# Router logits from the raw residual, with the scaled router weight stationary in four column groups

## The chip, the cores and the metric

The kernel runs on one core of one Trainium2 chip. It is one program that computes the whole two-layer encoder trunk. The metric is the device time of one execution in microseconds (us), as the median of three runs. TensorE is called PE, VectorE DVE, ScalarE ACT, GpSimd POOL and SyncE SP in the profile. PE does matrix products and writes them to PSUM; the other engines read PSUM and work on SBUF; SP and POOL start most transfers.

## The reference

There are 512 tokens of width 1024, and two layers. All is float32. A layer has an attention half and an expert half. What matters here is the end of the first half and the router at the head of the second:

```
x = x + g1 * hybrid_mixer(...)                        # residual after the mixer
h = rms_norm(x, norm2[l]) * (1.0 + sc2) + sh2         # x * rsqrt(mean(x*x) + EPS) * norm2, then scale and shift
scores = sigmoid(h @ w_router)                        # 512 x 16 experts, in 4 groups of 4
biased = scores + router_bias                         # best group by its two best, then the top 2 of it
gw = scores of the two chosen / their sum
each expert: (silu(xb @ w1[e]) * (xb @ w3[e])) @ w2[e]
x = x + g2 * (sum over the two chosen of gw * expert output)
```

`w_router` is 1024 x 16 and the same in both layers. The norm's gain, `sc2` and `sh2` are per channel; the reciprocal root of the mean square is per token. The experts' tokens are gathered by choice and multiplied with three weight tensors of 2 MB each.

## The kernel before, in words

Each engine has its own program, written out by hand, and the programs meet only at semaphores; an engine works its list strictly in order. Tokens are in four blocks (t = 0 to 3) of 128, one token to a partition; the 1024 channels are eight chunks of 128. Matrix products over channels need the tokens with channels on the partitions, so a block is transposed by PE against the identity, eight transposes into two PSUM banks of four, and copied from there to `hT`. The eight chunk transposes of a block are numbered in two counters, `tr_r` (transposed) and `tr_e` (read out of PSUM), which count in order.

*Around the change.* The last part of the attention half is the output product: eight products (k = 0 to 7, that is block t = k // 2, column half n = k % 2), each of eight matmuls of 128x512 (line 1871). Behind each, VectorE multiplies by the gate row and adds to the residual `x` (L1323, L1326), and counts `x1`. When both halves of a block are added:

- ScalarE squares the block and sums (L884; for the last block in two halves, L1031 and L1033), VectorE makes the mean (L1106), ScalarE takes the root (L888), VectorE the reciprocal `rstd` (L1111) and the normed block `xn` (L1113), and counts `xn_s`.
- PE transposes `xn` (L1630, called from L1875 or L1878). ScalarE evacuates it with the channel's scale and shift, one operation a chunk (L896); for the last block VectorE does the second four chunks (L1346).
- PE multiplies for the router: eight matmuls for a block, the block's 128 tokens stationary and the 16 columns of `wr` moving (L1855), into 16 columns of PSUM bank 2. The logits of block t-1 stand in PE's list behind product k = 2t + 1.
- POOL stores each `xn` block to DRAM (L818), waits for all four stores, then for the slot table, and gathers the tokens of the first expert pass (L826).

When all four blocks' logits stand in the bank, `lg_r` is counted. ScalarE takes the sigmoid of all 64 columns in one operation (L1040), VectorE chooses the experts, counts, ranks and makes the table of slots in some sixty small operations (L1359 to L1446), with small PE products in between. Then the gather, transposes and eleven expert passes follow (L1958, L1969). Each pass has 128 rows split into fixed tiles of 32, 64 or 128 rows, given to the experts by the rank of their counts; should an expert have more tokens than its tiles hold, a loop of extra blocks follows the passes.

*SP's queue* loads weights in a fixed order. In this stage: the first expert's weights while the output product runs; then it waits for the expert order (`ord_s`, L618), later for the first gather (L628), for `lg_r` (L634) before the load into `hT`, and for the stores of `xn` (L636) before the load into `reg_a`.

*Before this stage* VectorE's part of the gate loop (lines 1291 to 1317) runs eight rounds with PE and ScalarE. In layer 0 there are also small products for the next layer's modulation in PE's list behind the logits (L1889).

## Time and profile before

| | |
|---|---|
| median of 3 runs | 1590.02 us (1587.45 to 1592.77) |
| span of the profiled execution | 1586.8 us |
| profiled execution's own time | not recorded beyond its span |
| PE busy | 1485.2 us, 94% |
| DVE busy | 572.7 us, 36% |
| ACT busy | 438.6 us, 28% |
| POOL busy | 87.0 us, 5% |
| mean granted PE clock | 0.971 of full speed |
| router products of a block (L1855) | 16 records; 4 blocks, 2 layers |
| moved by DMA | 346.82 MB, mean 219 GB/s |

The profile is of one execution. The span runs from its first to its last instruction. A float32 matmul shows as two records. An engine's busy time says little by itself: what counts is the chain that ended last, followed back from the last instruction to what released it. "Issue" in a row is time in which an engine waited for nothing that the profile shows. The granted clock is the share of the full rate that PE was given in a stretch; 1.00 is 2.4 GHz and 0.50 is 1.2 GHz.

### The profile page before, as it was taken

The page shows a single profiled execution, that of the slowest core. Times are in us where ns is not written, and L with a number is a line of the kernel's source. Part 1 is how long each engine was busy: PE and PEld are TensorE (multiplying, and loading weights), DVE is VectorE, ACT ScalarE, POOL GpSimd, SP SyncE. Part 2 cuts the span into 40 slices and gives each one's busy share as a digit, 9 for nine tenths or more (in the row PEclk, how much of TensorE's full clock was granted, in tenths as well). Part 3 has the DMA queues.
Part 4 walks back from the last instruction along what each step waited for, and adds up shares of the span by engine and source line. Part 5 has one row for each costly group of instructions (what it writes and reads, how often), then busy time and mean ns, then how long its engine had stood idle before and what let it go on. Part 6 is the DMA issues. An engine that isn't in the chain of part 4 may idle for free.

```text
span 1586.8 us, 19587 instructions
## 1 busy us (share of the span) xinstructions
PE 1485.2 (94%) x7552; PEld 813.4 (51%) x7553; DVE 572.7 (36%) x1325; ACT 438.6 (28%) x1020; POOL 87.0 (5%) x96
## 2 busy tenths in 40 slices
PE   5998999999999789999989899999999949999996
PEld 1664555677755433444346555666775533334442
DVE  0056554566642401111154464464332250111115
ACT  2326565300013021211141565541010321121111
POOL 0000002000000001010000000110000000111000
PEclk8999999999999699999999999999999969999998
DMA  9626073225161699999962433401305139999994
GB/s 362 226 82 215 28 245 113 69 67 154 58 252 40 263 419 421 422 422 423 379 240 106 154 117 110 157 1 40 106 0 204 48 116 423 418 420 422 420 410 171
DMA packets 94872, 346.82 MB, mean 219 GB/s; under 512 B 13722, under 2 KB 37882, under 8 KB 80376
## 3 DMA queue, kind: packets, MB, share of 16 engines
q1 hardware_dynamic: 69152, 305.68, 49.2%
q0 software_dynamic: 8976, 31.45, 5.3%
q10 hardware_dynamic: 16648, 8.40, 1.8%
q8 instruction: 62, 1.02, 0.3%
q14 instruction: 34, 0.28, 0.1%
HBM read 331.54 MB, written 21.00 MB: 222 GB/s over the span
## 4 chain that ended last, share of the span: by engine, by line
PE 87%; DMA 5%; DVE 4%; ACT 2%; issue 1%; DVEq 1%; SPq 0%; POOLq 0%; ACTq 0%
PE bank L1958 18%; PE bank L1716 12%; PE bank L1666 10%; PE bank L1969 9%; PE bank L1758 7%; PE bank L1871 7%; PE bank L1773 5%; PE bank L1783 4%; PE bank L1793 4%; DMA ring<-in_w 2%; PE bank L1699 2%; PE bank L1597 2%; PE bank L1630 1%; DMA ring<-in_w_ada 1%; PE bank L1924 1%
## 5 line engine op out<-in xcount | busy, mean ns | idle before, releaser
L1958 PE MATMUL bank<-ring,reg_b 128*32 128x512 f32 (+2 forms) x1376 | 284.1, 607 | 2.9 <-ACT reg_b L1048 2.9
L1958 PEld LDWEIGHTS bank<-ring,reg_b 128*32 128x32 f32 (+2 forms) x1376 | 94.3, 129 | 141.1 <-issue 137.0
L1666 PE MATMUL bank<-ring,hT 128*128 128x512 f32 (+3 forms) x512 | 159.3, 472 | 2.4 <-ACT hT L896 2.4
L1666 PEld LDWEIGHTS bank<-ring,hT 128*128 128x128 f32 x512 | 97.8, 192 | 59.3 <-issue 32.4
L1969 PE MATMUL bank<-ring,reg_b 128*32 128x512 f32 (+2 forms) x576 | 127.3, 594 | 0.0
L1048 ACT ACTIVATE reg_b<-bank,cur 128x128 f32<-128x128 f32 x176 | 64.0, 470 | 180.3 <-PE bank L1924 180.3
L1758 PE MATMUL bank<-reg_a,ring 128*128 128x512 f32 x256 | 112.6, 593 | 0.9 <-issue 0.9
L1871 PE MATMUL bank<-ring,reg_b 128*128 128x512 f32 x256 | 112.2, 593 | 0.0
L975 ACT ACTIVATE reg_f<-bank,nmax 128x512 f32<-128x512 f32 x128 | 87.2, 684 | 61.2 <-DVE nmax L1258 60.1
L1258 DVE TENSOR_REDUCE nmax<-bank 128x1 f32<-128x512 f32 x128 | 83.8, 686 | 50.0 <-PE bank L1773 49.9
L1716 PE MATMUL bank<-hT,ring 128*128 128x256 f32 x384 | 88.1, 379 | 0.0
L1511 DVE TENSOR_TENSOR reg_d<-bank,reg_c 128x512 f32<-128x512 f32 x44 | 30.4, 692 | 145.5 <-PE bank L1969 145.5
L1716 PEld LDWEIGHTS bank<-hT,ring 128*128 128x128 f32 x384 | 72.8, 190 | 15.8 <-issue 6.7
L1501 DVE TENSOR_TENSOR reg_b<-bank,reg_b 128x512 f32<-128x512 f32 x22 | 15.2, 692 | 178.4 <-ACT reg_b L1055 178.4
L1793 PE MATMUL bank<-cst,reg_f 128*128 128x128 f32 x512 | 71.2, 281 | 6.7 <-DVE reg_f L1252 4.1
L1758 PEld LDWEIGHTS bank<-reg_a,ring 128*128 128x128 f32 x256 | 48.5, 190 | 55.6 <-issue 54.9
L1871 PEld LDWEIGHTS bank<-ring,reg_b 128*128 128x128 f32 x256 | 47.9, 190 | 56.4 <-issue 56.4
L1969 PEld LDWEIGHTS bank<-ring,reg_b 128*32 128x32 f32 (+2 forms) x576 | 41.4, 129 | 55.6 <-issue 54.9
L1252 DVE TENSOR_SCALAR reg_f<-reg_f,linv 128x512 f32<-128x512 f32 x128 | 66.2, 517 | 9.9
L1793 PEld LDWEIGHTS bank<-cst,reg_f 128*128 128x128 f32 x512 | 55.3, 141 | 26.3 <-DVE reg_f L1252 16.5
L896 ACT ACTIVATE hT<-bank,cur 128x128 f32<-128x128 f32 x120 | 43.7, 468 | 66.7 <-PE bank L1630 53.3
L1773 PE MATMUL bank<-reg_b 96*128 96x512 f32 x128 | 60.8, 603 | 0.0
(276 smaller groups left out, 1812.8 us busy)
## 6 DMA issues: line engine op xcount, KB each, us to landing
ring<-in_w SPq DMA_DIRECT2D x76, 2048.0 KB, 22.9
ring<-in_w_ada SPq DMA_DIRECT2D x19, 2048.0 KB, 8.0
ring<-in_w_in SPq DMA_DIRECT2D x10, 2048.0 KB, 19.3
hT<-in_w SPq DMA_DIRECT2D x10, 2048.0 KB
reg_a<-in_w SPq DMA_DIRECT2D x10, 2048.0 KB, 22.2
vb<-in_w_ada ACTq DMA_DIRECT2D x16, 512.0 KB, 4.0
ring<-in_w_o SPq DMA_DIRECT2D x4, 2048.0 KB, 8.7
ring<-in_w_proj_a SPq DMA_DIRECT2D x8, 512.0 KB, 10.8
```

The source lines that it names most:

```text
L975: A(prob[:, u % 2, h, :], bank[4 + at][:, :], ACT.Exp, bias=nmax[:, at:at + 1], accum_out=lsum[:, at:at + 1]).then_inc(ex_s, 1)
L1048: ins = A(xsT[:, b, cc, :], bank[(p0 + k) % 2][:, c * P:(c + 1) * P], ACT.Identity, scale=scale2(cc), bias=shift2(cc))
L1252: TS(prob[:, u % 2, h, :], prob[:, u % 2, h, :], linv[:, at:at + 1], None, ALU.mult).then_inc(pn_s, 1)
L1258: v.tensor_reduce(nmax[:, at:at + 1], bank[4 + at][:, :], X, ALU.max, negate=True).then_inc(mx_s, 1)
L1666: ins = pe.matmul(bank[z_bank(k)][:, 0:n], hT[:, c, t * P:(t + 1) * P], w[:, c, :], start=c == 0, stop=c == NC - 1)
L1716: ins = pe.matmul(bank[bk][:, half * 256:(half + 1) * 256], w[:, c, :], tokens[:, c, :], start=c == 0, stop=c == 3)
L1758: ins = pe.matmul(branch_bank(j, q)[:, :], w[:, c, (j % 4) * P:(j % 4 + 1) * P], oT[:, c + 4 * q, :], start=c == 0, stop=c == 3)
L1773: pe.matmul(bank[4 + 2 * (u % 2) + h][:, :], q_of(k, h), k_of(k, h), start=True, stop=True).then_inc(s_r, 1)
L1793: ins = pe.transpose(bank[2 + h][:, kc * P:(kc + 1) * P], prob[:, u % 2, h, kc * P:(kc + 1) * P], ident)
L1871: ins = pe.matmul(wo_bank(k)[:, :], mT[:, c, t * P:(t + 1) * P], w[:, c, :], start=c == 0, stop=c == NC - 1)
L1958: ins = pe.matmul(bank[bk][at:at + n, :], xsT[:, p % 2, c, at:at + n], slot(MOE_SLOT[j, m], NC, F)[:, c, :], start=c == 0, stop=c == NC - 1)
L1969: ins = pe.matmul(bank[6 + h][at:at + n, :], uT[:, c, at:at + n], slot(MOE_SLOT[j, 2], 4, D)[:, c, h * 512:(h + 1) * 512], start=c == 0, s ...
```

## The change

The logits are computed from the residual before its norm. With r the reciprocal root of a token, s and b the channel's scale and shift (s holds the norm's gain), the logits are r * (x @ (s * W)) + b @ W.

- VectorE makes `wr_g`, the router weight times the scale, 16 columns and 16 zero columns for each of the eight chunks, ahead of the gate loop, and the row sums of shift times weight, `wr_sum`, behind it. PE multiplies those by a matrix of ones after the first output product, which gives b @ W on every partition; VectorE copies it to `wr_c`.
- PE transposes `x` itself as soon as a block's residual is added. The copies to `hT` are now plain, of four chunks in one operation: ScalarE for all but the first half of the last block, which is VectorE's.
- The router product has the weight stationary, 32 columns wide, and the tokens moving, 128 columns. Chunk c goes to column group c % 4, so that a bank holds four partial sums on partitions 0, 32, 64 and 96. VectorE copies the 128x128 partials to SBUF. A second product with the partials stationary and a selection matrix of 16 columns (`sum_groups`, new constants) moving adds the four up and turns tokens back to partitions. VectorE then multiplies by r and adds `wr_c`. These steps are spread over the following products for blocks 0 to 2.
- The normed block is still made, for the gather. For blocks 0 to 2 VectorE does it as before; for the last block ScalarE does it, after the sigmoid. ScalarE's wait for `cur2_s` moves behind that.

```diff
+C_SEL = 812
-C_N = 812
+C_N = 828
...
+    for g in range(4):
+        c[32 * g:32 * g + E, C_SEL:C_SEL + E] = np.eye(E, dtype=np.float32)
...
+        logit_p = reg_d[:, 2048:2304].rearrange("p (b n) -> p b n", b=2)
+        logit = reg_d[:, 2304:2304 + NT * E].rearrange("p (t e) -> p t e", t=NT)
+        wr_g = reg_b[:, 4096:4352].rearrange("p (c n) -> p c n", c=NC)
...
 # SP
-                wait(sp, lg_r, l + 1)
+                wait(sp, lg_r, l * NT + NT)
...
 # ScalarE
-                act.wait_ge(cur2_s, l + 1)
+                def x_columns(t, k):
+
+                    act.wait_ge(tr_r, l * TR + TR_N2 + 2 * t + k + 1)
+                    A(hT[:, 4 * k:4 * k + 4, t * P:(t + 1) * P], bank[(TR_N2 + k) % 2][:, :].rearrange("p (c n) -> p c n", c=4),
+                      ACT.Copy).then_inc(tr_e, 1)
+
                 for t in range(NT):
                     if t == NT - 1:
                         act.wait_ge(sq_s, (l * 2 + 1) * NT + t)
                         act.wait_ge(x1, l * 8 + 2 * t + 1)
                         A(sq_j[:, 0:512], x[:, t, 0:512], ACT.Square, accum_out=ssq_h[:, 0:1]).then_inc(sqh_s, 1)
+                        for k in range(2):
+                            x_columns(t - 1, k)
                         act.wait_ge(x1, l * 8 + 2 * t + 2)
                         A(sq_j[:, 512:D], x[:, t, 512:D], ACT.Square, accum_out=ssq[:, t:t + 1]).then_inc(sq_s, 1)
+                        act.wait_ge(tr_e, l * TR + TR_N2 + 2 * t + 1)
+                        x_columns(t, 1)
                     else:
                         act.wait_ge(x1, l * 8 + 2 * (t + 1))
                         square(l * 2 + 1, t)
                     root(l * 2 + 1, t)
-                    modulated(l, TR_N2, t, scale2, shift2, chunks=1 if t == NT - 1 else 2)
-                act.wait_ge(lg_r, l + 1)
-                A(reg_f[:, 0:64], bank[2][:, 0:64], ACT.Sigmoid).then_inc(sc_s, 1)
+                    if t < NT - 2:
+                        for k in range(2):
+                            x_columns(t, k)
+                act.wait_ge(lg_s, l + 1)
+                A(reg_f[:, 0:64], logit.rearrange("p t e -> p (t e)"), ACT.Sigmoid).then_inc(sc_s, 1)
+                t = NT - 1
+                act.wait_ge(xr_s, l + 1)
+                A(xn[:, t, :], x[:, t, :], ACT.Identity, scale=rstd[:, t:t + 1]).then_inc(xn_s, 1)
+                act.wait_ge(cur2_s, l + 1)
...
 # VectorE: before the gate loop
+                v.memset(wr_g, 0.0)
+                v.drain()
+                TT(wr_g[:, :, 0:E], wr[:, :, :], cur[:, 3, :].unsqueeze(2).broadcast_to([P, NC, E]), ALU.mult)
...
 # VectorE: behind it
+                TT(wr_sh.rearrange("p (c e) -> p c e", e=E), wr[:, :, :], cur[:, 2, :].unsqueeze(2).broadcast_to([P, NC, E]), ALU.mult)
+                v.drain()
+                v.tensor_reduce(wr_sum, wr_sh.rearrange("p (c e) -> p e c", e=E), X, ALU.add).then_inc(wg_s, 1)
+
+                def copy_partial(t):
+
+                    v.wait_ge(lp4_r, l * NT + t + 1)
+                    v.tensor_copy(logit_p[:, t % 2, :], bank[3][:, t * P:(t + 1) * P]).then_inc(lp4_e, 1)
+
+                def finish_logits(t):
+
+                    v.wait_ge(lg_r, l * NT + t + 1)
+                    return STT(logit[:, t, :], logit_bank(t)[:, t * E:(t + 1) * E], rstd[:, t:t + 1], wr_c[:, :], ALU.mult, ALU.add)
...
                     TT(xs, xs, wo_t[:, k % 2, :], ALU.add).then_inc(x1, 1)
+                    if k == 0:
+                        v.wait_ge(lc_r, l + 1)
+                        v.tensor_copy(wr_c[:, :], bank[2][:, NT * E:(NT + 1) * E])
+                    if n == 0 and t >= 2:
+                        finish_logits(t - 2)
                     if n == 1:
+                        if t >= 1:
+                            copy_partial(t - 1)
                         if t == NT - 1:
                             v.wait_ge(sqh_s, l + 1)
                             TS(ssq_h[:, 0:1], ssq_h[:, 0:1], 1.0 / D, EPS, ALU.mult, ALU.add)
+                            v.wait_ge(tr_r, l * TR + (TR_N2 + 2 * t + 1))
+                            v.tensor_copy(hT[:, 0:4, t * P:(t + 1) * P], bank[TR_N2 % 2][:, :].rearrange("p (c n) -> p c n", c=4)).then_inc(tr_e, 1)
                             v.drain()
                             v.wait_ge(sq_s, (l * 2 + 1) * NT + (t + 1))
                             TS(ssq[:, t:t + 1], ssq[:, t:t + 1], 1.0 / D, ssq_h[:, 0:1], ALU.mult, ALU.add).then_inc(ms_s, 1)
+                            v.wait_ge(rt_s, (l * 2 + 1) * NT + (t + 1))
+                            v.reciprocal(rstd[:, t:t + 1], ssq[:, t:t + 1]).then_inc(xr_s, 1)
+                            copy_partial(t)
+                            v.drain()
                         else:
                             mean_square(l * 2 + 1, t)
-                        scaled(l * 2 + 1, t)
+                            scaled(l * 2 + 1, t)
...
-                v.wait_ge(tr_r, l * TR + (TR_N2 + 2 * NT))
...

+                for t in range(NT - 2, NT):
+                    ins = finish_logits(t)
+                ins.then_inc(lg_s, 1)
...
 # PE
-                def logits(t):
-                    for c in range(NC):
-                        if c % 4 == 0:
-                            pe.wait_ge(tr_e, l * TR + (TR_N2 + 2 * t + c // 4 + 1))
-                        ins = pe.matmul(bank[2][:, t * E:(t + 1) * E], hT[:, c, t * P:(t + 1) * P], wr[:, c, :],
-                                        start=c == 0, stop=c == NC - 1)
+                def x_transposes(t):
+
+                    pe.wait_ge(x1, l * 8 + 2 * (t + 1))
+                    xv = x[:, t, :].rearrange("p (q c) -> p c q", c=NC)
+                    for k in range(2):
+                        transposes(TR_N2 + 2 * t + k, [xv[:, 4 * k + c, :] for c in range(4)])
+
+                def partial_logits(t):
+
+                    for c in range(NC):
+                        if c % 4 == 0:
+                            pe.wait_ge(tr_e, l * TR + (TR_N2 + 2 * t + c // 4 + 1))
+                        ins = pe.matmul(bank[3][32 * (c % 4):32 * (c % 4) + 32, t * P:(t + 1) * P], wr_g[:, c, :], hT[:, c, t * P:(t + 1) * P],
+                                        start=c < 4, stop=c >= 4)
+                    ins.then_inc(lp4_r, 1)
+
+                def logits(t):
+
+                    pe.wait_ge(lp4_e, l * NT + t + 1)
+                    pe.matmul(logit_bank(t)[:, t * E:(t + 1) * E], logit_p[:, t % 2, :], sum_groups, start=True, stop=True).then_inc(lg_r, 1)
...
                     ins.then_inc(wo_r, 1)
+                    if k == 0:
+                        pe.wait_ge(wg_s, l + 1)
+                        pe.matmul(bank[2][:, NT * E:(NT + 1) * E], ones[:, :], wr_sum, start=True, stop=True).then_inc(lc_r, 1)
                     if n == 0 and t >= 1:
-                        norm_transposes(TR_N2, NT, t - 1)
+                        x_transposes(t - 1)
+                        if t >= 2:
+                            logits(t - 2)
                     if n == 1 and t >= 1:
-                        logits(t - 1)
-                norm_transposes(TR_N2, NT, NT - 1)
-                logits(NT - 1).then_inc(lg_r, 1)
+                        partial_logits(t - 1)
+                x_transposes(NT - 1)
+                logits(NT - 2)
+                partial_logits(NT - 1)
+                logits(NT - 1)
```

## Rows read from the trace of the kernel before

**Rows 1.** The page's summary of the chain that ended last, by engine.
```profile
PE 87%; DMA 5%; DVE 4%; ACT 2%; issue 1%; DVEq 1%; SPq 0%; POOLq 0%; ACTq 0%
```

**Rows 2.** Chain, layer 0, in order: start us, length us, what.
```profile
474.14 1.69 PE bank L1855 x16
...
500.08 6.88 PE bank L1871 x16
...
508.48 0.73 ACT reg_f L1033 x2
...
510.77 0.73 PE bank L1630 x4
...
513.08 3.61 PE bank L1855 x16
...
530.77 5.43 DMA reg_b<-xn_d,table
...
547.99 19.54 DMA ring<-in_w
```

**Rows 3.** Timeline, layer 1: start, length, engine, line, operation, [idle before <- releaser].
```profile
1275.89 0.69 DVE L1323 TENSOR_TENSOR reg_f<-bank,reg_c 128x512 f32<-128x512 f32 x1 [6.29 <-PE bank L1871]
...
1285.99 0.22 ACT L1040 ACTIVATE reg_f<-bank 128x64 f32<-128x64 f32 x1 [2.38 <-PE bank L1855]
```

**Rows 4.** By stretches: busy by engine (first three: PE alone), PEclk, DMA share, GB/s.
```profile
511.00:512.00 1.00, 0.93 (x8) 0.92 0.00 0
...
1279.00:1280.00 1.00, 0.33 (x2) 0.92 0.00 0
1280.00:1281.00 1.00, 1.00 (x7) 0.50 0.00 0
...
500.00:511.00 11.00, 8.87 (x35) 4.95 (x34) 3.27 (x7) 4.11 (x13) 0.00 (x0) 1.00 0.00 1
...
548.00:568.00 20.00, 15.78 (x144) 5.23 (x140) 2.08 (x3) 4.46 (x11) 0.99 (x1) 1.00 1.00 419
```

**Rows 5.** Timeline, PE alone: two column groups, then four, then full width.
```profile
286.71 1.09 PE L1783 MATMUL bank<-reg_b,vb 128*64 128x128 f32 x16
...
553.63 0.12 PEld L1958 LDWEIGHTS bank<-ring,reg_b 128*32 128x32 f32 x4 [0.31 <-issue]
...
574.10 0.63 PE L1958 MATMUL bank<-reg_a,reg_b 128*32 128x512 f32 x3
...
574.67 1.16 PE L1924 MATMUL bank<-cst,reg_b 128*128 128x128 f32 x8
```

**Rows 6.** Instructions by line: count, nanoseconds min/median/max, starts, forms.
```profile
L983 ACT ACTIVATE reg_b<-bank x64: 591/596/608, 133.5 to 1057.8; 128x512 f32<-128x512 f32 x64
...
L1263 DVE COPY reg_a<-bank x64: 279/292/293, 139.3 to 1074.5; 128x128 f32<-128x128 f32 x64
...
L1393 DVE SCALAR_TENSOR_TENSOR reg_f<-bank,cst x2: 175/175/175, 520.9 to 1290.2; 128x16 f32<-128x16 f32 x2
...
L1515 DVE COPY reg_d<-bank x2: 681/681/681, 606.5 to 1375.1; 128x512 f32<-128x512 f32 x2
...
L884 ACT ACTIVATE reg_f<-x x18: 1039/1056/1095, 18.5 to 1580.2; 128x1024 f32<-128x1024 f32 x18
```

**Rows 7.** Timeline, layer 0, ScalarE: a root's table load, the root, the sigmoid.
```profile
462.28 1.28 ACT L888 ACT_TABLE_LOAD   x1
...
463.57 0.20 ACT L888 ACTIVATE ssq<-ssq 128x1 f32<-128x1 f32 x1
...
516.71 0.22 ACT L1040 ACTIVATE reg_f<-bank 128x64 f32<-128x64 f32 x1 [2.38 <-PE bank L1855]
```

**Rows 8.** Timeline, layer 0, VectorE: first gate product's sum; first output product.
```profile
307.11 0.42 DVE L1295 TENSOR_TENSOR ring<-bank,reg_f 128x256 f32<-128x256 f32 x1 [1.13 <-ACT reg_f L1019]
...
452.76 0.69 DVE L1323 TENSOR_TENSOR reg_f<-bank,reg_c 128x512 f32<-128x512 f32 x1 [5.48 <-PE bank L1871]
```

**Rows 9.** DMA issues, 500 to 570: buffers, queue, count, median us to landing.
```profile
xn_d<-reg_a POOLq DMA_DIRECT2D x1, 512.0 KB, 2.9
```

More of the change, by code:

```diff
@@ L252, in trunk @@
         ident = cst[:, C_ID:C_ID + P]
+        sum_groups = cst[:, C_SEL:C_SEL + E]
         utri_b = cst[:, C_UT:C_UT + P // 2].bitcast(b16)
@@ L371, in branch_bank, with logit_bank @@
             return bank[((2, 3), (7, 1))[j % 2][q]]
+        def logit_bank(t):
+            return bank[2 if t < NT - 1 else 3]
         def wo_bank(k):
@@ L443, in trunk @@
         xn_st = sem("normed_stored")
+        wg_s = sem("router_weights_scaled")
+        lc_r = sem("logits_of_shift_ready")
+        xr_s = sem("last_block_reciprocal_root_ready")
+        lp4_r, lp4_e = sem("partial_logits_ready"), sem("partial_logits_copied")
         lg_r = sem("logits_ready")
+        lg_s = sem("logits_scaled_and_shifted")
         sc_s = sem("router_scores")
```

11 lines of the change are left out of this document (3 added, 8 removed).

## The prediction

> **What bounds the kernel now.** I read the page's summary of the chain first [rows 1]: TensorE (PE) is 87% of the chain that ended last, so time is saved either by giving PE less to do or where the chain leaves PE. Then the chain in order of time through the edited stage of layer 0 [rows 2]. Up to 507.0 us PE runs the eight output products without a pause, and things are slotted between them: eight transposes per token block, the router product of blocks 0 and 1 (1.69 each; the row of block 0 stands for both), and that of block 2, which overlaps VectorE's work on the last product and is on nobody's path. At 506.96 (500.08 + 6.88) the last product ends; I call this moment M. From M the chain hops: the residual add, final at M + 1.50; the square sum; root, reciprocal and normed block; its transposes (M + 3.81); the modulation in four operations of ScalarE; the 16 records of the last router product from 513.08 on, 3.61; and the sigmoid at 516.71, M + 9.75 [rows 2, 7]. Layer 1 has the same with M = 1275.86 and the sigmoid at 1285.99, M + 10.13 [rows 3]. After the sigmoid comes a fixed chain of small VectorE operations up to the gather at 530.77, then a wait for expert weights, 547.99 to 567.53 [rows 2].
>
> The granted clock, by stretches [rows 4]: 1.00 (2.4 GHz) up to 511; the stretch 511 to 512 has 0.92, so it fell to 0.50 (1.2 GHz) near 511.8, and in layer 1 near 1279.8, both after the gap in which PE waited for the normed block. The last router product runs wholly at the low level: 3.61 us for what costs 1.69 in the stream.
>
> **The change, part by part.**
>
> *Router product inside the stream.* Removed from the chain: 2 x 1.69 = 3.38 us a layer. Added: partial logits of blocks 0 and 1, and three single products of 16 columns (the shift's logits after the first output product, and the folding of the four groups for blocks 0 and 1). A float32 matmul is two records. A partial is 8 matmuls, 16 records, stationary 32 wide, moving 128 wide, on four column groups. No such shape is in the trace; the neighbours are the expert product, where four groups of 512 columns start together every 0.43 us, and the attention's value product on two groups of 64 with 128 moving columns, 16 records in 1.09 us, pairs starting 0.11 apart [rows 5]. Four groups together with 128 columns would be 4 x 0.11 = 0.43 at best; the four weight loads took 0.12, so I take 0.12 a quad, 0.50. Going from column groups to full width shows as 574.10 to 574.67, 0.57 where the cadence is 0.43 [rows 5]: 0.14, and I estimate as much for the way in; together 0.25. That makes 0.75 a partial. A single product is two records at 0.11 (16 records took 1.69): 0.22. Per layer: 3.38 - 2 x 0.75 - 3 x 0.22 = **1.22 saved**. Bounds: partial at 0.43 without switches, +1.86; groups strictly one after another, 16 x 0.11 plus switches = 2.0 each, -1.28 (a loss). I take the middle value, since both neighbours show groups overlapping.
>
> The Trainium skill (TensorEngine Tiling (Array Packing), Key Properties) says that changing the tiling mode drains TensorE, which speaks against putting 32-wide products between full ones. The 0.14 at 574 agrees with a drain, and says that it is small; without the switches the sum would be 1.0 us better over two layers.
>
> *After M.* The normed block no longer stands before the transposes. By hops, with M = 0:
> - Residual add final at 1.50, as now. PE transposes the raw block at once (partial of block 2 ended near 0.75): first four done 0.73 later, as now [rows 2], at 2.26.
> - VectorE: copy of block 2's partial, 0.29 (the attention's 128x128 copy [rows 6]), the small mean operation, then the first half of the transposes, 128x512 from PSUM at 0.68 [rows 6]: 2.28 to 2.96.
> - ScalarE: second square 1.52 to 2.23, as now. Then it waits for VectorE's half (the counter is kept in order) and copies its own, 0.60 [rows 6]: 2.98 to 3.58. Behind this wait stands the root, which would have been ready at 3.25: 3.60 to 3.80.
> - PE: first half of the partial meanwhile, second half from 3.62; two quads and the latency of one matmul (0.27, which is 1.09 less 15 starts of 0.055 [rows 5]): 4.05.
> - VectorE copies the partial, 0.29: 4.36. PE folds: weights, two records, latency, 0.5: 4.88. VectorE's multiply-add 0.175 (128x16 out of PSUM [rows 6]): 5.1. Sigmoid at about 5.1 if all is at 2.4 GHz.
> - The clock fell at M + 4.9 in layer 0 and M + 4.1 in layer 1. Low for the partial and the fold adds 0.6 at most. I take 5.4.
> - ScalarE's table load for the sigmoid now starts behind the root, not behind the modulation: 3.82 + 1.28 = 5.10 [rows 7]. It was covered by the router product (ScalarE waited 2.38 more after it [rows 7]); now it is level with the chain, and a floor.
>
> So the sigmoid comes at M + 5.4 in place of 9.75 and 10.13: **4.35 and 4.73 saved**. Bounds: 5.1 (the floor), and 7.0 with serial groups at the low clock (8 x 0.22 for half a partial and 0.8 for the fold).
>
> The Trainium skill (ScalarE: Activation LUTs, What ACT_TABLE_LOAD costs) gives 1283 ns for the load and a drain of about 1380 ns more at each change of set. By that the sigmoid would come at 3.8 + 2.66 = M + 6.5. The trace has the 1.28, but no drain: at 462.28 the load starts, and the root runs 1.29 later [rows 7].
>
> *Costed at nothing.* (a) The clear, drain and multiply that build the scaled weight, about 0.7, at the head of the gate loop: VectorE sits idle there for 1.13 until ScalarE's copy [rows 8]. (b) The shift's product and reduction after the loop, about 0.6, fall into 5.48 of idle [rows 8]; PE asks for them only after the first output product. Without cover each costs its own length. (c) The normed last block is now a ScalarE pass after the sigmoid, 128x1024, 1.06 as the squares are [rows 6], so it starts at M + 5.6, not M + 3.0. POOL's queue waits for it with the fourth store, 2.9 us to landing [rows 9], and behind that stand the wait for all stores and the gather. Landed by M + 10.2; the gather starts 14.06 after the sigmoid (516.71 to 530.77), M + 19.5. Nine microseconds of room; the cost of losing them is one for one. (d) SP's loads move with the logits: one waits on them, but stands in the queue behind the gather and so moves as the gather does. (e) In the middle blocks VectorE gains a copy and a small multiply-add, and loses nothing; it sits idle for 5.48 before the first product [rows 8] and in like manner before the next ones, and PE's products after the fourth ask only for residual adds three products old. ScalarE's modulations of four operations become one copy of 0.60 each. (f) Sixteen more constant columns: nothing measurable.
>
> *Sum.* 2 x 1.22 + 4.35 + 4.73 = 11.5 us. Everything behind the sigmoid hangs on it: the expert order, the gather and the loads they release. Against the profiled execution, whose span is 1586.8 us (nothing outside the span is recorded for it), that makes 1575.3. The median of the runs is 1590.0, 3.2 above the span, so I forecast **1578.5 us**. With both bounds the gain lies between 13.4 (2 x 1.86 + 4.65 + 5.03) and 3.3 (-2 x 1.28 + 2.75 + 3.13).
>
> **Rivals.**
> 1. *The column groups run one behind another.* For: the new groups read four different moving tiles in the shape with the fewest columns, where starting costs weigh most. Against: the expert product also reads different tiles, three from one buffer and one from another, and its quads start together [rows 5]. Gain 3.3, time 1586.7.
> 2. *ScalarE becomes the bound after M.* The square, the ordered copy, the root and the table load are in one line there. If that line runs one pass of 128x1024 (1.06 [rows 6]) later than I count, the sigmoid is at M + 6.5: 1.1 lost a layer, gain 9.3, time 1580.7. For it: six things must follow each other without a gap. Against it: each of them is in the trace of now with gaps of 0.02 to 0.3. The drain that the Trainium skill gives (above) would end at the same M + 6.5.
> 3. *The gain is given back at the expert weights.* For: the chain holds 19.54 us of waiting for a load after the first expert pass [rows 2], and the transfers are at 1.00 of their engines there [rows 4], so a stage bound by transfers could take the slack. Against: all loads in that queue wait for the expert order or the gather, both later than the sigmoid, and nothing is in flight around M (0.00 from 500 to 511 [rows 4]). Gain 0 to 2, time near 1589.
> 4. *Slower: a token changes its expert.* The logits are rounded in another order. An expert block whose rows are exactly full in the static tiling would then overflow, and the extra block runs unoverlapped at the end of a layer: three weight tensors of 2 MB, some 15 us at the stage's 419 GB/s [rows 4]; with a gather of 5.4 as on the chain [rows 2] and products that I estimate at 21 (48 records of 0.43 for the three weight tensors), 40 us. It decides from one token beyond a full tile; nothing of such a block is in the chain of now. Time about 1618. Float32 rounding seldom turns a choice, so it gets little.
>
> **How the numbers follow.** Forecast 0.72, rival 1 0.08, rival 2 0.08, rival 3 0.07, rival 4 0.05. A measurement can tell about 0.3% here, 4.8 us. Faster than that: the forecast, rival 2, and the part of rival 1 where groups overlap in part, 0.83. Within: the rest of 1 and rival 3, 0.12. Slower: 0.05. The range begins at the upper bound of the gain, 1590.0 - 13.4 = 1576.6, less 3 for the spread of the runs (their lowest is 2.6 below their median), 1573.5, and goes to 1585.5, which takes in rival 2 and half of rival 1.
>
> **What would show it.** In the profile after: router matmuls of 128*32 between the output products, 16 records in about 0.75; M about 1.2 earlier; sigmoid at M + 5.4, the table load ending just before; the fourth store behind the sigmoid, and the gather still waiting for the table; PE's wait for weights near 19.5 as before. Wrong if a partial takes 1.5 or more, if the sigmoid waits for ScalarE's table, if the gather is released by a store, or if products of an extra block run.

## The result and the profile after

The changed kernel takes 1577.62 us (median of 4 runs, 1576.05 to 1581.49) against 1589.30 (4 runs, 1587.45 to 1592.77) for the kernel before on the same chip: ratio 0.9932, 95% interval 0.9917 to 0.9947. That is 11.7 us between the medians; 1578.5 was forecast. The profiled execution has a span of 1576.5, against 1586.8 before. Run again later, beside the experiments, the changed kernel gave 1578.35 (4 runs), ratio 0.9937 [0.9921, 0.9954]. Brackets behind a ratio are its 95% interval; the ratios are taken over the runs and are not exactly those of the medians.

The page's summary of the chain reads as before [rows 1]: a gain of less than 1% doesn't move these shares, and the stage has to be read itself.

```profile
PE 87%; DMA 5%; DVE 4%; ACT 2%; issue 1%; DVEq 1%; SPq 0%; POOLq 0%; ACTq 0%
```

The chain of waits of the changed kernel, layer 0 (start, length, what), answers [rows 2]:

```profile
453.12 0.13 PE bank L1946 x2
453.25 13.83 PE bank L1941 x32
...
467.95 6.87 PE bank L1941 x16
474.82 0.57 PE bank L1920 x16
475.40 7.07 PE bank L1941 x16
...
483.35 0.13 PE bank L1927 x2
...
499.10 6.98 PE bank L1941 x16
...
507.62 0.73 PE bank L1687 x4
508.37 0.70 DVE hT L1390
509.09 0.61 ACT hT L1048
509.74 0.47 PE bank L1920 x8
510.23 0.30 DVE reg_d L1363
510.57 0.41 PE bank L1927 x2
511.01 0.24 DVE reg_d L1368
511.27 0.27 ACT reg_f L1070
...
525.35 5.74 DMA reg_b<-xn_d,table
...
543.51 18.21 DMA ring<-in_w
...
570.45 7.00 PE bank L2046 x64
```

The partial logits are L1920, 0.57 where the router product had 1.69; L1941 is the output product, L1946 the shift's single product, L1927 the folding of the groups. The last output product ends at 499.10 + 6.98 = 506.08: this is M. The sigmoid (L1070) comes at 511.27, M + 5.19. Layer 1, in its timeline, has the same: the sum begins 0.02 behind M, so M = 1270.27, and the sigmoid is at M + 5.19 again.

```profile
1270.29 0.69 DVE L1374 TENSOR_TENSOR reg_f<-bank,reg_c 128x512 f32<-128x512 f32 x1 [6.38 <-PE bank L1941]
...
1275.46 0.26 ACT L1070 ACTIVATE reg_f<-reg_d 128x64 f32<-128x64 f32 x1 [0.20 <-DVE reg_d L1368]
```

| | before, layer 0 / 1 | after, layer 0 / 1 | saved | forecast |
|---|---|---|---|---|
| first output product to M | 61.34 / 61.33 | 59.99 / 59.99 | 1.35 + 1.34 | 1.22 + 1.22 |
| M to the sigmoid | 9.75 / 10.13 | 5.19 / 5.19 | 4.56 + 4.94 | 4.35 + 4.73 |
| sum | | | 12.2 | 11.5 |

The timeline of layer 0 (start, length, engine, line, operation; idle before and its releaser in brackets) answers [rows 7, 9]:

```profile
509.80 1.28 ACT L1070 ACT_TABLE_LOAD   x1
...
511.27 0.26 ACT L1070 ACTIVATE reg_f<-reg_d 128x64 f32<-128x64 f32 x1 [0.20 <-DVE reg_d L1368]
...
513.14 0.53 POOL L837 DMA_DIRECT2D xn_d<-reg_a  x1 [17.46 <-ACT reg_a L1073]
...
525.35 1.09 POOL L845 DMA_INDIRECT reg_b<-xn_d,table  x1 [11.68 <-DVE table L1503]
```

ScalarE's wait of 2.38 behind the table load has shrunk to 0.20. The norm of the last block now runs behind the sigmoid and its store is issued at 513.14, but the gather was released by the table (L1503), 14.08 after the sigmoid, where it was 14.06 before: the moved store costs nothing.

The granted clock of PE, by stretches (busy, share, clock, DMA share, GB/s), answers [rows 4]:

```profile
510.00:511.00 1.00, 0.59 (x11) 1.00 0.00 0
511.00:512.00 1.00, 1.00 (x5) 0.67 0.00 0
```

It fell to its lower level (1.2 GHz) after 511, when the logits were done (PE's part of them ended at 510.98). Before, the last router product ran wholly under that level.

The spans differ by 10.3, not 12.2. Places on the two time axes tell where the rest went. The first output product of layer 0 begins 0.47 later (446.09 against 445.62), so its sigmoid is 5.44 earlier and not 5.91; the 0.47 is already there at 136 us, ahead of anything that the change touches. The first transposes of layer 1 are 5.85 earlier, the products behind them only 3.95; the sigmoid of layer 1 is 10.53 earlier. So 1.90 is lost between two neighbouring groups of instructions at the layer boundary; smaller differences, 0.41 ahead of it and 0.30 behind it, go the other way. The chain at the boundary, after and then before:

```profile
797.43 1.97 PE bank L1687 x8
799.40 2.81 PE bank L1669 x4
802.21 4.29 PE bank L1723 x10
```

```profile
803.28 1.16 PE bank L1630 x8
804.44 1.72 PE bank L1612 x4
806.16 4.29 PE bank L1666 x10
```

The same twelve records take 4.78 in place of 2.88, under a granted clock of 0.50 in place of 1.00. Whether the change does that was the first open question for the experiments.

Such differences are as large ahead of the stage: in the fourteen profiles of this document the first output product of layer 0 begins at anything from 443.54 to 446.36 (445.62 and 446.25 in the two of the kernel before, 446.09 and 443.97 in the two of the changed one). So the stage is read from its own start and from M, not from places on the time axis.

### The profile page after: what moved, and what is told of

Read it like the earlier page. It is cut to its first block, busy times and chain, and to the rows that moved or that the text cites. A ratio compares the mean times of both kernels' runs of the same rounds, so it can differ in the third digit from the quotient of the medians.

```text
span 1576.5 us, 19611 instructions
## 1 busy us (share of the span) xinstructions
PE 1476.3 (94%) x7572; PEld 801.5 (51%) x7573; DVE 575.3 (36%) x1343; ACT 427.8 (27%) x980; POOL 86.9 (6%) x96
## 4 chain that ended last, share of the span: by engine, by line
PE 87%; DMA 5%; DVE 4%; ACT 2%; issue 1%; DVEq 1%; SPq 0%; POOLq 0%; ACTq 0%
PE bank L2035 18%; PE bank L1773 12%; PE bank L1723 10%; PE bank L2046 9%; PE bank L1941 7%; PE bank L1815 7%; PE bank L1830 5%; PE bank L1840 4%; PE bank L1850 4%; DMA ring<-in_w 2%; PE bank L1756 2%; PE bank L1654 2%; PE bank L1687 2%; PE bank L2001 1%; DMA ring<-in_w_ada 1%
## 5 line engine op out<-in xcount | busy, mean ns | idle before, releaser
L2046 PE MATMUL bank<-ring,reg_b 128*32 128x512 f32 (+2 forms) x576 | 127.3, 594 | 0.0
L1941 PE MATMUL bank<-ring,reg_b 128*128 128x512 f32 x256 | 113.0, 596 | 0.0
L1558 DVE TENSOR_TENSOR reg_b<-bank,reg_b 128x512 f32<-128x512 f32 x22 | 15.2, 691 | 179.3 <-ACT reg_b L1089 179.3
L1941 PEld LDWEIGHTS bank<-ring,reg_b 128*128 128x128 f32 x256 | 47.7, 190 | 56.3 <-issue 56.3
L2046 PEld LDWEIGHTS bank<-ring,reg_b 128*32 128x32 f32 (+2 forms) x576 | 41.4, 129 | 55.6 <-issue 54.9
L1561 DVE TENSOR_TENSOR reg_b<-bank,reg_b 128x512 f32<-128x512 f32 x22 | 15.2, 692 | 124.0 <-PE bank L2035 124.0
```

What stands on the lines that cost most here:

```text
L1941: ins = pe.matmul(wo_bank(k)[:, :], mT[:, c, t * P:(t + 1) * P], w[:, c, :], start=c == 0, stop=c == NC - 1)
L2046: ins = pe.matmul(bank[6 + h][at:at + n, :], uT[:, c, at:at + n], slot(MOE_SLOT[j, 2], 4, D)[:, c, h * 512:(h + 1) * 512], start=c == 0, s ...
```

## The experiments

Theory: the gain is 2 x 1.35 from partial products that overlap in four column groups, and 4.56 + 4.94 from the shorter way behind M; both halves are needed. Rivals: one half brings all of it; the groups don't overlap; ScalarE's line bounds the end; the boundary takes part of it back. Each kernel is the changed one with the edit shown, unless said otherwise.

### Each half alone

**Raw residual, no groups.** The raw block is transposed as in the changed kernel, but the router product is the old one, tokens stationary and 16 columns moving; no copy and no folding.

```diff
-                        ins = pe.matmul(bank[3][32 * (c % 4):32 * (c % 4) + 32, t * P:(t + 1) * P], wr_g[:, c, :], hT[:, c, t * P:(t + 1) * P],
-                                        start=c < 4, stop=c >= 4)
+                        ins = pe.matmul(logit_bank(t)[:, t * E:(t + 1) * E], hT[:, c, t * P:(t + 1) * P], wr_g[:, c, 0:E],
+                                        start=c == 0, stop=c == NC - 1)
...
-                            copy_partial(t - 1)
...
-                            logits(t - 2)
```

> Half of the change: raw residual transposed, scaled weight, root and shift on the 16 logits, but the tokens stationary as before (8 products of 128x16, no column groups, no partial copy, no folding). Theory: the gain behind the last output product comes from taking the norm out of the line, the groups only save PE time in the stream. Then per layer the stream keeps its 2 x 1.69 and pays 0.13 for the shift product, and the sigmoid comes at M + 5.1 or so, no later than in the changed kernel (half a product, 8 x 0.11 + 0.27, in place of 0.47 + 0.30 + 0.41 for partial, copy and folding), with the table load at M + 5.0 as a floor. Gain 4.65 + 5.0 - 0.3 = 9.4 us of 11.7, ratio 0.9941. Rival (the groups bring the gain, because the product at the end falls from 3.61 to 0.9): without them the sigmoid is at M + 7.5 and the gain under 6, ratio above 0.996.

Measured: 1582.24 (4 runs), ratio 0.9953 [0.9937, 0.9970]: by the ratio 7.5 less than the 1589.6 of the kernel before in these runs, where 9.4 was expected. The stream is 0.2 longer than before; the sigmoid is at M + 5.30 in layer 0 but M + 6.49 in layer 1. Timeline of layer 1 (M = 1273.65), then PE's stretches there:

```profile
1276.68 3.15 PE L1917 MATMUL bank<-reg_b,hT 128*128 128x16 f32 x16 [0.34 <-DVE hT L1388]
...
1280.14 0.26 ACT L1070 ACTIVATE reg_f<-reg_d 128x64 f32<-128x64 f32 x1 [1.49 <-DVE reg_d L1368]
```

```profile
1276.00:1277.00 1.00, 0.66 (x7) 1.00 0.00 0
1277.00:1278.00 1.00, 1.00 (x8) 0.60 0.06 16
```

The clock fell under the last product, and its 16 records took 3.15, where they took 1.97 in layer 0. That is 1.2 of the 1.9 that the expectation missed; the hops and the stream of both layers make up about 0.5 more. Where the clock did not fall early, the sigmoid is at M + 5.30, only 0.11 behind the whole change: behind M the groups save little in hops.

They go together with a later fall. In the three profiles with the tokens stationary (the kernel before twice, and this one) the clock falls 3.6 to 4.9 behind M, in both layers of each, before the last router product is over. In the eleven with the weight stationary it falls 5.2 or more behind M in every layer read, and in every version of the whole change the logits are done by then. PE's wait for the normed block does not decide this: this kernel lacks it and its clock falls early, the next one has it and its clock falls at M + 5.5 and M + 5.9. Which property of the router product does is not shown.

**Groups, norm first.** Built on the kernel before: normed block, modulated evacuation, then partial logits in four groups and the folding.

```diff
-                        ins = pe.matmul(bank[2][:, t * E:(t + 1) * E], hT[:, c, t * P:(t + 1) * P], wr[:, c, :],
-                                        start=c == 0, stop=c == NC - 1)
+                        ins = pe.matmul(bank[3][32 * (c % 4):32 * (c % 4) + 32, t * P:(t + 1) * P], wr_g[:, c, :], hT[:, c, t * P:(t + 1) * P],
+                                        start=c < 4, stop=c >= 4)
```

> The other half: column groups, partial copy and folding, but the norm first and the modulation in the evacuation as before, root, scale and shift on the tokens. Theory: the line M, add, square, root, normed block, transposes, modulation stays as it was to M + 6.6; then half a partial at the low clock 0.7, copy 0.30, folding 0.6 to 0.8, sigmoid at M + 8.3 against 9.75. Stream saves 1.35 a layer less the shift product, 1.5. Gain 2 x (1.5 + 1.5) = 6 us, ratio 0.9962. Together with the first half it is more than the whole (9.4 + 6 against 11.7), since both shorten the same last router product. Rival (groups bring the gain): 9 us or more, ratio under 0.9943.

Measured: 1583.56 (6 runs), ratio 0.9967 [0.9955, 0.9980]: 5.2 by the ratio, about the 6 that was expected. From the first output product to M it is 59.8. Timeline of layer 0, M = 503.31:

```profile
503.33 0.69 DVE L1339 TENSOR_TENSOR reg_f<-bank,reg_c 128x512 f32<-128x512 f32 x1 [6.52 <-PE bank L1896]
...
511.57 0.22 ACT L1048 ACTIVATE reg_f<-bank 128x64 f32<-128x64 f32 x1 [0.91 <-PE bank L1882]
```

M + 8.26 was expected (8.3) and came. The halves together are 12.7, more than the whole gave beside them (10.0 by its ratio). Both shorten the same last router product of 3.61, which can be saved only once; that this is the whole of the 2.7 is argued, and the intervals alone could hide as much. Neither half alone is the change.

**The changed kernel again**, as it is, beside these three.

> The changed kernel again, on the same chip as the three others, as what they are compared with. All theories: ratio 0.9932 within 0.0015; sigmoid at M + 5.19 in both layers. If the clock at the layer boundary (794 us in the first profile of it, where 1.9 us were given back) falls at another time in this execution, that loss is chance and not the change.

Measured: 1578.35 (above), sigmoid at M + 5.19 and M + 5.20, and 1.97 for the boundary's first transposes again.

**All chunks in one column group.** The same records, one behind another.

```diff
-                        ins = pe.matmul(bank[3][32 * (c % 4):32 * (c % 4) + 32, t * P:(t + 1) * P], wr_g[:, c, :], hT[:, c, t * P:(t + 1) * P],
-                                        start=c < 4, stop=c >= 4)
+                        ins = pe.matmul(bank[3][0:32, t * P:(t + 1) * P], wr_g[:, c, :], hT[:, c, t * P:(t + 1) * P],
+                                        start=c == 0, stop=c == NC - 1)
```

> The changed kernel with all eight chunks in one column group, accumulated one behind another in 32 PSUM partitions; the rest (copy, folding) kept. It takes away the overlap of the groups alone and so prices the first rival of the prediction. Theory: a partial is 16 records of 128 columns one behind another, 16 x 0.11 = 1.75 us against the 0.57 measured, so 2 x 1.2 lost in the stream and 0.45 at the end, per layer 2.9, both 5.7 us: ratio 0.9932 + 0.0036 = 0.9968. Rival (starting and weight loading, not streaming, set the pace, so that groups save nothing): no difference from the changed kernel, ratio 0.9932.

Measured: 1584.43 (7 runs), ratio 0.9968 [0.9957, 0.9979]. Its chain, layer 0 (M = 507.11):

```profile
473.30 1.86 PE bank L1921 x16
...
510.40 1.95 PE bank L1921 x16
...
513.41 0.27 ACT reg_f L1070
```

The ratio is the expected one. In the profile each partial in the stream takes 1.86 in place of 0.57, and the sigmoid is at M + 6.3, 1.1 later where 0.45 was expected, since all 16 records were on the chain behind M (1.95) and not only half of them. With the 2.55 that the stream is longer, that is 3.7 a layer where 2.9 was expected, more than the ratio shows. By the ratios, overlap of the groups is worth half of the whole gain (0.0031 of 0.0063). Rival 1 is refuted: this kernel is what it described, and the changed one is faster.

### What sets the sigmoid behind M

**Own semaphores for the last two copies.** ScalarE no longer waits for VectorE's copy to keep one counter in order. VectorE's copy gets a semaphore of its own too, and PE waits for the two; these lines are left out here.

```diff
-                      ACT.Copy).then_inc(tr_e, 1)
+                      ACT.Copy).then_inc(xa_s if t == NT - 1 else tr_e, 1)
...
-                        act.wait_ge(tr_e, l * TR + TR_N2 + 2 * t + 1)
```

> The changed kernel with a semaphore of its own for each of the two last copies to hT, so that ScalarE no longer waits for VectorE's half. Theory (each hop behind M is on the line, this wait too): ScalarE copies from M + 2.75, when the second four transposes are done, to 3.35, not from 3.02; the second half of the partial starts 0.3 earlier; the root too, so the table load ends near M + 4.75. Sigmoid at M + 4.9 against 5.20, 0.6 us less over both layers (too little for the time to show). Rival (the line is held by the root and the table load, not by the logits): it moves as well, since both stand behind the same wait, but then the load ends just at the sigmoid, without the 0.15 to 0.2 of idle before it.

Measured: one run, 1576.86. Timeline, layer 0, M = 504.26:

```profile
504.28 0.69 DVE L1374 TENSOR_TENSOR reg_f<-bank,reg_c 128x512 f32<-128x512 f32 x1 [6.38 <-PE bank L1944]
...
507.80 1.28 ACT L1070 ACT_TABLE_LOAD   x1
...
509.18 0.26 ACT L1070 ACTIVATE reg_f<-reg_d 128x64 f32<-128x64 f32 x1
```

The sigmoid is at M + 4.92 (4.93 in layer 1), 0.27 earlier a layer: the ordered counter was on the path. The load ends at 509.08 and ScalarE's idle time has gone; VectorE's last multiply-add on the logits ends at 509.14. So the table load is now level with the logits. One run can't tell 0.5 us of the time.

**No table load.** A square in place of the sigmoid; the scores and so the chosen experts are others than the reference's.

```diff
-                A(reg_f[:, 0:64], logit.rearrange("p t e -> p (t e)"), ACT.Sigmoid).then_inc(sc_s, 1)
+                A(reg_f[:, 0:64], logit.rearrange("p t e -> p (t e)"), ACT.Square).then_inc(sc_s, 1)
```

> The changed kernel with a square in place of the router's sigmoid, which needs no other function table there; the choice of experts is then another one, so only the line up to that operation is read, not the time of the run. It takes the table load of 1.28 away alone. Theory: the load ends at M + 5.01, the last logits at M + 5.17, so the load is hidden by 0.1 to 0.2 and the operation still starts at M + 5.2. Second rival of the prediction (ScalarE is the bound, or a drain follows the load): it starts at M + 5.0 or earlier, or the multiply-add of VectorE before it moves.

Timeline, layer 0 (M = 506.36):

```profile
506.38 0.69 DVE L1374 TENSOR_TENSOR reg_f<-bank,reg_c 128x512 f32<-128x512 f32 x1 [6.38 <-PE bank L1941]
...
511.57 0.26 ACT L1070 ACTIVATE reg_f<-reg_d 128x64 f32<-128x64 f32 x1 [1.50 <-DVE reg_d L1368]
```

The square starts at M + 5.21, as the sigmoid does, and ScalarE waited 1.50 for the logits: the table load is hidden in the changed kernel. The time of this kernel, 1817.32, says nothing on that: with other experts the static tiles overflow and extra expert blocks run, two in each layer. It does say that overflow is dear: some 240 us here, 60 a block with all that stands around it.

**Norm before the sigmoid.** The 128x1024 pass and with it the fourth store come first, so that the gather no longer waits for that store if it did, and ScalarE's line ahead of the sigmoid is one pass longer.

```diff
-                act.wait_ge(lg_s, l + 1)
-                A(reg_f[:, 0:64], logit.rearrange("p t e -> p (t e)"), ACT.Sigmoid).then_inc(sc_s, 1)
...
+                act.wait_ge(lg_s, l + 1)
+                A(reg_f[:, 0:64], logit.rearrange("p t e -> p (t e)"), ACT.Sigmoid).then_inc(sc_s, 1)
```

> The changed kernel with ScalarE's pass for the last normed block ahead of the sigmoid, not behind it. Theory (ScalarE's line root, pass, table load, sigmoid would then end last): the pass runs from M + 3.95 to 5.05, the table load to 6.35, sigmoid at M + 6.4 against 5.20, 1.2 later in each layer; the store of the block is 1.3 earlier and nobody gains by that. Rival (the store behind the sigmoid is what holds the gather): the gather starts earlier against the sigmoid, under 14.0 us behind it.

Measured: one run, 1578.52. Timeline, layer 0, M = 504.53:

```profile
508.45 1.15 ACT L1071 ACTIVATE reg_a<-x,rstd 128x1024 f32<-128x1024 f32 x1 [0.23 <-DVE rstd L1395]
...
509.62 1.28 ACT L1073 ACT_TABLE_LOAD   x1
...
510.91 0.26 ACT L1073 ACTIVATE reg_f<-reg_d 128x64 f32<-128x64 f32 x1
...
525.00 1.09 POOL L845 DMA_INDIRECT reg_b<-xn_d,table  x1 [14.29 <-DVE table L1503]
```

The sigmoid is at M + 6.38, 1.2 later, and the gather 14.09 behind it although the store was issued 0.74 before the sigmoid. So the gather hangs on the sigmoid, and by this line the order chosen in the change is the right one; the time of one run can't show it. This kernel has what rival 2 described, ScalarE's line ending last; the changed one doesn't.

### The 1.9 us at the layer boundary

**The kernel before, again.**

> The kernel before once more, for a second profile of it. Asked: was its full clock at 803 us, through the eight transposes and the last pass of block 2 of the layer boundary, its rule or its luck? All six profiles of kernels with the change or a part of it had 0.50 there. If it has 0.50 here as well (eight transposes 1.97 and not 1.05 to 1.16), the 1.9 us of difference between the first two profiles are a difference of executions and not of kernels, and the change gave nothing back. If it is at 1.00 again, the change does give something back at the boundary. I think the first, six to four. Sigmoids at M + 9.75 and M + 10.13 within 0.5.

Measured: 1589.68, one run. Its chain at the boundary:

```profile
804.35 1.97 PE bank L1630 x8
806.32 2.81 PE bank L1612 x4
```

The kernel before also has 1.97 and 2.81, the lower level, which its first profile did not have. So the 1.9 is a difference that two executions of one kernel show, and does not need the change. Whether the change makes the lower level there more likely is not shown: the kernel before has it in one profile of two, the changed kernel and its variants without extra products in all nine. The sigmoids of this profile are at M + 10.15 and M + 9.93, where the first had 9.75 and 10.13: the saving behind M would be 9.7 with them, not 9.5.

**Ten, then five, products of 384 columns that feed nothing**, ahead of the boundary's transposes, to hold the clock up. The edit with five:

```diff
+                    for i in range(5):
+                        pe.matmul(bank[5][:, 0:384], ident, cst[:, C_CA:C_CA + 384], start=True, stop=True)
```

> The changed kernel with ten products of 384 columns that nobody reads, into a free PSUM bank, in PE's list at the layer boundary behind the added-up last pass of blocks 0 and 1 (3.2 us at the full clock), where PE waits 4.9 us for the normed block. Theory: of the 12.1 us that the two sigmoids came earlier in the first profiles, 1.9 were lost at 797 to 802, where the clock was at 0.50 in the changed kernel and at 1.00 in the one before; with PE kept working the clock stays at 1.00, the eight transposes take 1.0 and not 1.97, the last pass of block 2 takes 1.72 and not 2.4 to 2.8. Gain 1.5 to 1.9 us on the changed kernel, ratio to before 0.9922. Rival (the clock falls there whatever PE does, or the time is made up behind it, where PE waits for weights): no gain, ratio 0.9935; if the extra products run at 0.50 they take 6.4 us and delay the transposes, ratio up to 0.9945.

> As b2_keep_clock, but five extra products, not ten: the ten took 6.45 us at full clock, since a product of 384 columns is two records of 0.32, and held the transposes back by 3 us. Five take 3.2 and end before the normed block. Theory: clock 1.00 through the boundary as in b2, transposes 1.0, last pass of block 2 1.72, nothing delayed; 1.5 to 2 us less than the changed kernel: ratio to before 0.9923. Rival (the pause of a microsecond or two left behind the extra products is enough to lose the clock, or the next stage waits for weights anyway): ratio 0.9935.

Ten: 1579.12 (5 runs), ratio 0.9940 [0.9920, 0.9959]. I had counted one record for each product, they are two: the ten took 6.45 on the chain and held the transposes back by 3 (800.38 against 797.43). Five: 1577.61 (4 runs), 0.9928 [0.9912, 0.9943], the same as the changed kernel. The chain with five at the boundary, and then, from layer 0, its first product behind the wait for weights (7.07 in the changed kernel):

```profile
797.47 0.94 PE bank L1687 x8
798.41 1.72 PE bank L1669 x4
```

```profile
561.39 8.69 PE bank L2037 x64
```

The clock was 1.00 through the transposes and the group behind them, as with ten, though it had been 0.50 from about 790 to 793.4, ahead of the extra products. What follows came 2.1 earlier than in the changed kernel (800.13 against 802.21). The time is no better, and the two profiles tell where the 2.1 went: the first output product of layer 1 begins 0.82 earlier (1209.46 against 1210.28), and the expert product behind that layer's wait for weights begins at 1325.73 in both, the wait being 18.66 and not 17.85. The 8.69 in layer 0 is a matter of the clock, 0.50 from 562 to 564 where the changed kernel has 1.00, and no work of the extra products, which run 230 us later. With the own semaphores besides:

> The changed kernel with both edits: a semaphore for each of the last two copies (sigmoid at M + 4.93 in b1) and the five extra products at the layer boundary. Theory: 0.55 and 1.5 to 2 us, together 2.3 less than the changed kernel, ratio to before 0.9918. Rival as for e1_keep_clock_5: only the 0.55, ratio 0.993.

Measured: 1578.97 (5 runs), 0.9934 [0.9920, 0.9947], where 0.9918 was expected; sigmoid at M + 4.93 in both layers, the boundary at full clock, and again a slow product at the same place in layer 0, 8.77, with the clock at 0.51 from 562 to 564. I found no version that is measurably faster than the changed kernel.

### Loads ahead of the gather

**The tensor `w3` of the second expert is loaded before SP waits for the gather.** It is meant to shorten the wait for weights of 18.21.

```diff
-                wait(sp, xg_s[0], l * (16 * gathers(0)) + 16)
                 wait(sp, wo_r, l * 8 + 8)
                 load_w3(1, rank[1])
+                wait(sp, xg_s[0], l * (16 * gathers(0)) + 16)
```

> The changed kernel with the load of expert 1's second weight tensor issued before SP's wait for the first gather, not behind it. It asks what bounds the stretch from the gather to 562 us, where the chain holds 18.2 to 19.5 us of waiting for weights. Theory: that stretch is bound by the transfers (six tensors of 2 MB from the gather on at 420 GB/s), and only their start counts; started 4.5 us earlier, while the gather leaves a part of the transfers idle (360 GB/s of 420), the wait shrinks by 1 to 2 us a layer, less what the gather becomes slower: ratio 0.992. Rival (weights and gather share the transfers, so the gather is delayed by what is won): the gather's landing moves from 5.7 to 9 us, and the ratio stays 0.9935 or gets worse.

Measured: 1582.26 (6 runs), ratio 0.9962 [0.9949, 0.9974], slower than the changed kernel by 4. Its chain, layer 0:

```profile
523.73 10.35 DMA reg_b<-xn_d,table
...
536.90 16.04 PE bank L2035 x128
...
572.04 7.00 PE bank L2046 x64
```

The wait of 18.21 is gone from the chain, but the gather takes 10.35 in place of 5.74 (6.28 in the changed kernel's second profile). The load is issued at 519.99, 3.7 ahead of the gather, and the transfers are at 0.97 to 1.00 of their engines from 522 to 532. From the gather's start to the start of the L2046 pass it is 48.31, against 45.10 and 46.44 in the two profiles of the changed kernel. The load's wait for the gather is worth keeping. The expectation's rival was right here, its theory wrong.

## Why the prediction was right

*Term 1, the router product inside the stream: forecast 1.22 a layer, measured 1.35 and 1.34.* The bounds were -1.28 and +1.86. By the chain, partial and the product behind it take 0.57 + 7.07 where they took 1.69 + 6.96: 1.01 saved each, forecast 0.94. A single product adds 0.13 itself and 0.10 to the one behind it (13.83 for the two products behind it, where the chain has 6.87 for one behind the transposes): 0.23, forecast 0.22. 2 x 1.01 - 3 x 0.23 = 1.33. The Trainium skill (TensorEngine Tiling (Array Packing), Key Properties) says that a change of tiling mode drains TensorE. The rows agree that something is paid, and that it is small: the partial takes 0.57, where four groups at 0.11 would take 0.43, and the output product behind it 7.07, where it took 6.96 behind the old router product. Together that is 0.25 a partial above the 0.43, where the forecast had 0.32 (0.25 for the switches, 0.07 for the weight loads): 0.68 against 0.75. The rows don't tell the two apart.

*Term 2, after M: forecast M + 5.4, measured 5.19 in both layers.* The hops, forecast then measured, from M = 506.08: last residual add final 1.50, 1.49; four transposes done 2.26, 2.27; VectorE's copy begun 2.28, 2.29; ScalarE's copy done 3.58, 3.61; copy of the partial begun 4.05, 4.15; folding begun 4.36, 4.49; sigmoid 5.1, 5.19. What the forecast had on top, half of the 0.6 for a low clock, did not come: the clock fell after the logits, at M + 5.3 and M + 5.7, not at the M + 4.9 and M + 4.0 of before (the prediction's 4.1 for layer 1 doesn't follow from its own 1279.8). The prediction saw both falls after the gap in which PE waited for the normed block, which is gone. The two kernels with half of the change speak against that gap as the cause: one has no such gap and falls at M + 3.6 in layer 1, the other has it and falls at M + 5.5. Why the fall came later stays open, and that the logits escaped it is in part luck.

*Costed at nothing.* (a) and (b), layer 0: the weight's preparation took VectorE's idle time at the gate loop from 1.13 [rows 8] to 0.48 in the row of the same sum, with ScalarE still its releaser, and the shift's product and reduction took the wait ahead of the first output product from 5.48 [rows 8] to 4.83:

```profile
307.57 0.42 DVE L1332 TENSOR_TENSOR ring<-bank,reg_f 128x256 f32<-128x256 f32 x1 [0.48 <-ACT reg_f L1038]
```

(c): the store and the gather as forecast. (d) and rival 3: the wait for expert weights is 18.21, from 19.54 [rows 2] (19.05 and 18.38 in the second profiles, so these waits show no effect of the change). From the sigmoid to the first L2046 product, L1969 before, it is 59.18, from 59.56 before, and 60.54 and 59.43 in the second profiles: the stage behind moves with the sigmoid within about 1 us, and did not take the gain back. (e): VectorE's sum after the last output product had waited 6.38 for PE, as 6.29 before [rows 3]; VectorE gives PE nothing late. Rival 4: no products of an extra block run (19611 instructions, against 21785 in the kernel with the square, where such blocks do), and the price that I gave a block, 40 us, is near: there, the gathers of the first two blocks start 42.88 apart (801.66 and 844.54). Table work around the blocks comes on top.

*The sum.* 12.2 against 11.5 by the hops, 11.7 by the medians. The result lies 0.9 from the forecast, less than the spread of the runs. The two terms and their mechanism were right; that the time is as close as this is partly luck: a profiled execution differs from its neighbour by 1.9 at the layer boundary alone.

The Trainium skill (ScalarE: Activation LUTs, What ACT_TABLE_LOAD costs) adds a drain of about 1380 ns to the 1283 ns of a load. The 1283 agree (1.28). The drain does not show: with the norm first, the load begins 0.02 behind the pass ahead of it, ends at 510.90, and the sigmoid starts at 510.91. Hence the M + 6.5 that this rule gave did not come in the changed kernel (5.19); without the load, the operation starts at the same M + 5.21.

What stays open: whether the lead at the boundary is always spent in layer 1's wait for weights, as in the one profile with five extra products, and why both profiles with five have the low clock behind that wait in layer 0. Each is one execution, and no run separates cause from chance. Whether the copies' own semaphores bring their 0.5 us also needs more runs than were made.

## What to carry to other kernels

When a stage ends in a chain over several engines, take out of it what can be applied to the small result instead: here the norm and the shift worked on 1024 channels, ahead of their transposes and their product, and now work on the 16 logits. Count such a change as hops from the last long product, and ask for each engine what stands ahead in its queue. Before a difference of 1 or 2 us between two profiles is put down to a change, profile the kernel before a second time.

## What the runs showed of the hardware

- Eight float32 products with a 128x32 stationary and 128 moving columns take 0.57 in four column groups and 1.86 in one, between full-width products.
- The granted clock is at its lower level in some executions of one kernel and not in others at the same place: 1.16 and 1.97 for the same eight transposes of the kernel before.
- Behind M the clock fell after 3.6 to 4.9 us in six layers with 128 token columns stationary in the router product, and after 5.2 us or more in twenty-one with 32 weight columns stationary. The reason is not shown.
- With five extra products of 384 columns ahead of them the transposes ran at the full clock (0.94 and 1.16 for the eight in two kernels, 1.72 in place of 2.81 for the next group), without a gain in the time.
- A 2 MB load issued 3.7 us ahead of a gather stretched the gather from 5.74 to 10.35, and in layer 1 from 5.51 to 9.35.
- With the norm first, the table load of 1.28 cost ScalarE's line nothing beyond itself: it began 0.02 behind the operation ahead of it, and the operation behind it started 0.01 after its end.
